# A hybrid decoder step on one core: TensorE's branch for extra pairs ahead of the last pair's second gates, and another order of the last combination

## The chip, the cores and the metric

One core of one Trainium2 chip runs the whole program. The metric is the device time of one execution in microseconds. Before the change three runs took 1240.19, 1240.31 and 1242.56 us; their median is 1240.31 us. The engines are TensorE (PE, its weight loads PEld), VectorE (DVE), ScalarE (ACT), GpSimd (POOL) and SyncE (SP), which here issues the transfers. Each engine has a sequencer that reads its instructions, queues those that the engine executes, and itself executes reads of a register, branches and drains.

## The reference

One step of a decoder layer, for 256 prompt tokens and 32 sample tokens (8 sequences of 4) of width 1024: RMSNorm and one input projection, retention and block-sparse attention beside each other, an output projection and residual, then RMSNorm, a router and 32 experts, of which each token uses 4, another residual, and a last RMSNorm. All of it is in float32. What the change touches is the end of this part:

```python
def expert(acc, xs):
    wgu, bgu, wd, bd, g = xs
    u = tok @ wgu + bgu
    glu = jnp.minimum(u[:, ::2], SWIGLU_LIMIT)
    lin = jnp.clip(u[:, 1::2], -SWIGLU_LIMIT, SWIGLU_LIMIT)
    a = glu * jax.nn.sigmoid(SWIGLU_ALPHA * glu) * (lin + 1.0)
    return acc + g[:, None] * (a @ wd + bd), None
...
return hres + moe(rmsnorm(hres, norm2_g), ...)
...
y_prompt = rmsnorm(yp, final_norm_g)
y_sample = rmsnorm(ys, final_norm_g)
```

## The kernel before

The experts are worked off in 16 pairs. A pair gathers up to 64 tokens for each of its two experts (xt), multiplies them by the gate and up weights ("gates": four parts of 2 MB an expert, 16 matmul instructions a part in the trace), applies the clamped product, and multiplies by the down weights (two parts an expert). The result (out2) is brought back to token rows by a matmul with the weighted one-hot matrix sgt (the combination). SP issues the weight loads, one part of 2 MB each, into a ring of 9 slots; each load waits until the slot's former part has been used.

Pairs 0 to 14 run in a loop on each engine (`pe.Fori` at L1150, three pairs a pass). The last pair has its own function, `last_pair`: the first expert's gates (L1078), the combination of the pair before (`combine`: units 2 and 3 at L955, the sample rows at L959) with the turn of the first expert's product between (`turn_a`, L974), three transposes of the one-hot matrix (L1113), then the second expert's gates (L1078 again, `gates(1)`). What remains is in `finish`: the down matmuls (L1094), the turn of the second expert's product, and `place_y`, which puts part of the residual into PSUM.

If more than 64 tokens chose one expert, extra pairs have to run. Their number is known only on the chip, so every engine reads it (`extra_pairs`, L430 to L433: a wait and a register load from the arena, `TENSOR_LOAD`) and branches on it. On TensorE the branch stands at L1155, between `gates(1)` and `finish`; `finish` is there in both bodies of it. In the run profiled here the number is 0 and the Else body (L1167) is taken.

Behind the branch comes `combine_last`: TensorE adds the last pair's results to the residual in PSUM, in banks of their own. The 32 sample rows are laid as four quarters of 256 columns on 128 rows; their sum of squares is first added up by ScalarE for each quarter, and a matmul with `same_row` (L1005) adds the four quarters of a row. ScalarE squares and adds up (L1486, L1492) and takes roots (`root_last`, L1482); its functions come from table sets, loaded by `ACT_TABLE_LOAD`, which the compiler inserts. VectorE takes the reciprocal (L2007), multiplies by it and by the gains (L2009, L2015), and SP stores: four transfers for the quarters (L2231), one for token tile 0 (L2235), two halves for tile 1 (L2238).

What sets the order: every engine works its own list of instructions, in the order written; semaphores hold an engine until another has come so far. There is no planner.

Of the kernel before, what the change touches and what calls it, by code (L numbers as in the profile page):

```python
# [26 lines left out]
ACT = mybir.ActivationFunctionType  # L27
AXX = mybir.AxisListType.X

P = 128  # L30
D = 1024
# [140 lines left out]
def build_kernel(nc, t, table, outs):  # L172

    with ExitStack() as ctx:
# [7 lines left out]
        psum = ctx.enter_context(nc.psum_tensor("psum", [P, 8, 512], F32))  # L182

        def at(start, *dims):

            flat = arena[:, start:start + int(np.prod(dims))]
            if len(dims) == 1:
                return flat
            names = "abcd"[:len(dims)]
            return flat.rearrange(f"p ({' '.join(names)}) -> p {' '.join(names)}",  # L190
                                  **dict(zip(names, dims)))
# [48 lines left out]
        HT = cur; cur += 2304  # L240
# [54 lines left out]
        f_gain = at(SR + 3072, D)  # L295
# [4 lines left out]
        gain_quarters = at(SR + 2048, 256)  # L300
# [13 lines left out]
        gates = at(MX + 2048 + TILES * (E + 2), TILES, E + 2)  # L314
        assert 2048 + 2 * TILES * (E + 2) <= 2304
        squares = at(HT, D)

        def token_sum(tile):
            a, b = TAIL_BANKS[tile]
            return psum[:, a:b + 1, :]  # L320

        y_out = hn
# [118 lines left out]
        def _(pe):  # L441
# [544 lines left out]
            def combine_last(m):  # L986

                pe.wait_ge(sgt_ready, m + 1)
                pe.wait_ge(out_ready, m * 2 + 1)
                pe.wait_ge(out_half, 1)  # L990
                pe.wait_ge(y_placed, 3)

                def token_tile(tile, half):
                    return mm(psum[:, TAIL_BANKS[tile][half], :], sgt[:, P * tile:P * (tile + 1)],
                              out2[:, 512 * half:512 * (half + 1)], start=False, stop=True,
                              skip_group_check=True)

                for j in range(4):
                    last = mm(psum[NS * j:NS * (j + 1), 0, 0:256], sgt[:, 2 * P:2 * P + NS],
                              out2[:, 256 * j:256 * (j + 1)], start=False, stop=True,  # L1000
                              skip_group_check=True)
                last.then_inc(final_full, 1)
                token_tile(0, 0)
                pe.wait_ge(sq_quarters, 1)
                mm(psum[:, 5, 0:1], same_row, stat[:, 52:53],  # L1005
                   start=True, stop=True).then_inc(final_full, 1)
                token_tile(0, 1).then_inc(final_full, 1)
                token_tile(1, 0)
                token_tile(1, 1).then_inc(final_full, 1)

            def pair(n, landed, ahead):
# [52 lines left out]
            def last_pair(n, landed):  # L1064

                pe.wait_ge(xt_ready, n + 1)
                pe.wait_ge(esel_ready, n + 1)

                def gates(e):
                    lhs = slice(SLOTS * e, SLOTS * (e + 1))  # L1070
                    for kk in range(4):
                        slot, value = landed(4 * e + kk)
                        pe.wait_ge(wt_in[slot], value)
                        for m in range(2):
                            for b in range(2):
                                for g in range(2):
                                    c = 1024 * g + 512 * b
                                    last = mm(psum[64 * g:64 * (g + 1), 6 * e + b, :], xt[:, 2 * kk + m, lhs],  # L1078
                                              gate_slot[slot][:, m, c:c + 512], start=False,
                                              stop=kk == 3 and m == 1, skip_group_check=True)  # L1080
                        last.then_inc(w_used, 1)

                def down(e, q):
                    slot, value = landed(8 + 2 * e + q)
                    if e == 1 and q == 1:
                        pe.wait_ge(half_in, 16)
                    else:
                        pe.wait_ge(wt_in[slot], value)
                    a_t = at_last if e else at_sb
                    for m in range(4):  # L1090
                        if e == 1 and q == 1 and m == 2:
                            pe.wait_ge(wt_in[slot], value)
                        for g in range(2):
                            last = mm(psum[64 * g:64 * (g + 1), 1 if e else 2, :],  # L1094
                                      a_t[:, m, SLOTS * q:SLOTS * (q + 1)],
                                      down_slot[slot][:, m, 512 * g:512 * (g + 1)],
                                      start=q == 0 and m == 0, stop=q == 1 and m == 3)
                    last.then_inc(w_used, 1)

                bias(n, 0)  # L1100
                gates(0)
                pe.wait_ge(sgt_ready, n + 1)
                pe.wait_ge(out_ready, n * 2 + 1)
                combine(n, range(2))
                for b, g in ((0, 0), (1, 1), (0, 1), (1, 0)):
                    mm(psum[64 * g:64 * (g + 1), 6 + b, :], esel[E * b:E * (b + 1), 1, :],
                       bgu[E * b:E * (b + 1), g, :], start=True, stop=False, skip_group_check=True)
                turn_a(n, 0)
                combine(n, range(2, 5))
                pe.wait_ge(selg_ready, n + 1)  # L1110
                pe.wait_ge(u_read, n * 2 + 2)
                for tile in range(3):
                    last = tr(psum[:, 0, P * tile:P * (tile + 1)],  # L1113
                              selg[:, tile].rearrange("p a b -> p (a b)"), ident)
                last.then_inc(sgt_full, 1)
                gates(1)

                def finish():
                    pe.wait_ge(at_ready, n * 2 + 1)
                    down(0, 0)  # L1120
                    turn_a(n, 1)
                    place_y(n + 1, ((0, 0),))
                    down(0, 1)
                    pe.wait_ge(at_ready, n * 2 + 2)
                    down(1, 0)
                    down(1, 1)

                return finish
# [44 lines left out]
        def _(act):  # L1173
# [307 lines left out]
            def root_last(tile, total):  # L1481
                nc.scalar.activation(stat[:, 53 + tile:54 + tile], total, ACT.Sqrt,  # L1482
                                     scale=1.0 / D, bias=const("eps")).then_inc(sq_ready, 1)

            act.wait_ge(final_full, 1)
            nc.scalar.activation(squares[:, 0:256], psum[:, 0, 0:256], ACT.Square,  # L1486
                                 accum_out=stat[:, 52:53]).then_inc(sq_quarters, 1)
            act.wait_ge(final_full, 2)
            root_last(2, psum[:, 5, 0:1])
            for tile in range(2):  # L1490
                act.wait_ge(final_full, 3 + tile)
                link(nc.scalar.activation(squares.rearrange("p (a b) -> p a b", a=2), token_sum(tile), ACT.Square,  # L1492
                                          accum_out=stat[:, 50 + tile:51 + tile]))
                root_last(tile, stat[:, 50 + tile:51 + tile])


        @block.vector
        def _(dve):
# [505 lines left out]
            def final_norm(n, tile, dst, src, gains):  # L2004
                dve.wait_ge(sq_ready, n + 1)
                r = stat[:, 53 + tile:54 + tile]
                v.reciprocal(r, r).then_inc(f_rstd, 1)  # L2007
                dve.wait_ge(f_rstd, n + 1)
                v.scalar_tensor_tensor(dst, src, r, gains, ALU.mult, ALU.mult).then_inc(yo_ready, 1)  # L2009

            halves = lambda a: a.rearrange("p (a b) -> p a b", a=2)
            final_norm(0, 2, y_out[:, 2, 0:256], psum[:, 0, 0:256], gain_quarters)
            final_norm(1, 0, halves(y_out[:, 0, :]), token_sum(0), halves(f_gain))
            final_norm(2, 1, y_out[:, 1, lo], psum[:, TAIL_BANKS[1][0], :], f_gain[:, lo])
            v.scalar_tensor_tensor(y_out[:, 1, hi], psum[:, TAIL_BANKS[1][1], :], stat[:, 54:55], f_gain[:, hi],  # L2015
                                   ALU.mult, ALU.mult).then_inc(yo_ready, 1)
# [89 lines left out]
        def _(sp):  # L2106
# [119 lines left out]
            with sp.Else():  # L2226
                sp.nop()

            sp.wait_ge(yo_ready, 1)
            for j in range(4):  # L2230
                sp.dma_start(outs[1].rearrange("s i d -> (s i) d")[:, 256 * j:256 * (j + 1)],  # L2231
                             y_out[NS * j:NS * (j + 1), 2, 0:256]).then_inc(stored, 16)
            out_p = outs[0][0].rearrange("(t p) d -> p t d", p=P)
            sp.wait_ge(yo_ready, 2)
            sp.dma_start(out_p[:, 0, :], y_out[:, 0, :]).then_inc(stored, 16)  # L2235
            for half in range(2):
                sp.wait_ge(yo_ready, 3 + half)
                sp.dma_start(out_p[:, 1, 512 * half:512 * (half + 1)], y_out[:, 1, 512 * half:512 * (half + 1)])\  # L2238
# [30 lines left out]
```

## Time and profile before

| | |
|---|---|
| profiled execution, in all | 1238.33 us |
| its span | 1236.5 us |
| TensorE matmul, busy | 1195.6 us (97%), 7264 instructions |
| TensorE weight load, busy | 507.2 us (41%) |
| VectorE, busy | 389.5 us (32%) |
| ScalarE, busy | 234.0 us (19%) |
| moved by DMA | 500.64 MB, mean 405 GB/s |
| chain that ended last | TensorE 66%, DMA 21%, VectorE 8%, issue 4%, ScalarE 1% |

Times in the views count from the start of the span. A row of the timeline has start, length, engine, line, operation, output and input, the count of instructions merged into it, and in brackets the idle time before it and what ended it. A matmul's end is modelled, and matmuls overlap, so a group's length is not count times mean. A q behind an engine's name (PEldq, ACTq, SPq) marks its sequencer. The granted clock of TensorE is a share of full speed: 1.00 is 2.4 GHz, 0.50 is 1.2 GHz.

### The profile page before, as it was taken

What the parts mean: (1) busy time and instruction counts of PE and PEld (TensorE: products, weight loads), DVE (VectorE), ACT (ScalarE), POOL (GpSimd) and SP (SyncE); (2) the same over time, 40 slices, a digit from 0 to 9 for tenths busy, and PEclk for the clock granted to TensorE, in tenths of its full rate; (3) what the DMA queues carried; (4) which work ended last, traced back from release to release, by engine and by line L of the source; (5) the groups of instructions that cost most, each with busy time, mean ns of one, the idle gap of its engine ahead of it and who ended that gap; (6) DMA issues with size and microseconds to landing.
All of it is one profiled execution on the core that took longest, in us unless ns stands there. A gap on an engine that the chain in (4) does not pass through costs nothing.

```text
span 1236.5 us, 17233 instructions
## 1 busy us (share of the span) xinstructions
PE 1195.6 (97%) x7264; PEld 507.2 (41%) x7264; DVE 389.5 (32%) x554; ACT 234.0 (19%) x521; POOL 68.0 (6%) x70
## 2 busy tenths in 40 slices
PE   7999999999999999999999999999999999999996
PEld 3555544535443434344343434343343434343432
DVE  4999956464311111222111111112111111111113
ACT  4021145304111101021211101021202111111103
POOL 2222202230000000000000000000000000000000
PEclk9999999999999999999999999999999999999999
DMA  8999889999999999999999999999999999999995
GB/s 333 369 363 361 332 326 389 382 363 385 381 414 427 428 428 428 429 428 428 430 427 430 427 429 428 428 429 428 429 428 429 429 428 430 428 428 430 426 430 233
DMA packets 49978, 500.64 MB, mean 405 GB/s; under 512 B 5656, under 2 KB 6320, under 8 KB 19088
## 3 DMA queue, kind: packets, MB, share of 16 engines
q1 hardware_dynamic: 42416, 430.56, 83.3%
q0 software_dynamic: 7520, 69.47, 14.2%
q8 instruction: 32, 0.52, 0.2%
q14 instruction: 10, 0.08, 0.0%
HBM read 495.29 MB, written 4.72 MB: 404 GB/s over the span
## 4 chain that ended last, share of the span: by engine, by line
PE 66%; DMA 21%; DVE 8%; issue 4%; ACT 1%; SPq 0%; DVEq 0%; ACTq 0%
PE psum L1027 24%; DMA arena<-w_gate_up 18%; PE psum L1058 14%; PE psum L935 6%; DVE arena L1556 5%; DMA arena<-w_down 3%; PE psum L533 3%; PE psum L955 3%; PE psum L941 2%; PE psum L967 2%; PE psum L624 2%; PE psum L753 2%; PE psum L453 2%; PE psum L974 1%; PE psum L1094 1%
## 5 line engine op out<-in xcount | busy, mean ns | idle before, releaser
L1027 PE MATMUL psum<-arena 128*64 128x512 f32 x1920 | 421.7, 594 | 11.8 <-DMA arena<-w_gate_up 11.8
L1027 PEld LDWEIGHTS psum<-arena 128*64 128x64 f32 x1920 | 135.0, 137 | 294.9 <-issue 267.5
L1899 DVE TENSOR_SCALAR arena<-psum 128x512 f32<-128x512 f32 x32 | 22.2, 692 | 675.2 <-PE psum L1027 635.9
L1058 PE MATMUL psum<-arena 128*64 128x512 f32 x960 | 212.6, 595 | 0.0
L1184 ACT ACTIVATE arena<-psum 128x512 f32<-128x512 f32 (+4 forms) x192 | 97.6, 511 | 350.4 <-PE psum L1058 170.6
L1556 DVE STREAM_TRANSPOSE arena<-arena 128x2048 f32<-128x2048 f32 x32 | 121.4, 3926 | 2.1 <-PE psum L518 1.9
L1058 PEld LDWEIGHTS psum<-arena 128*64 128x64 f32 x960 | 66.2, 136 | 124.3 <-issue 122.5
L533 PE MATMUL psum<-arena 128*128 128x512 f32 x224 | 107.7, 618 | 0.4 <-ACT arena L1184 0.4
L1429 ACT ACTIVATE arena<-arena 128x512 f32<-128x512 f32 x30 | 18.9, 631 | 412.5 <-DVE arena L1899 412.5
L1184 ACT ACTIVATE arena<-psum,arena 128x128 f32<-128x128 f32 (+2 forms) x162 | 49.3, 404 | 174.1 <-PE psum L533 113.7
L935 PE MATMUL psum<-arena 128*128 128x128 f32 x512 | 76.8, 293 | 0.2 <-DVE arena L1811 0.2
L935 PEld LDWEIGHTS psum<-arena 128*128 128x128 f32 x512 | 66.4, 199 | 16.7 <-issue 12.7
L955 PE MATMUL psum<-arena 128*128 128x512 f32 x128 | 63.6, 618 | 0.0
L533 PEld LDWEIGHTS psum<-arena 128*128 128x128 f32 x224 | 40.2, 192 | 47.2 <-issue 46.6
L1922 DVE TENSOR_TENSOR arena<-psum,arena 128x512 f32<-128x512 f32 (+1 forms) x80 | 48.0, 633 | 12.6 <-PE psum L955 12.6
L518 PE MATMUL psum<-arena 128*32 128x128 f32 x1024 | 35.4, 280 | 6.7 <-DVE arena L1575 3.8
L518 PEld LDWEIGHTS psum<-arena 128*32 128x32 f32 x1024 | 26.7, 111 | 31.5 <-DVE arena L1556 16.2
L2039 POOL DMA_INDIRECT arena<-cache_k,arena x32 | 32.4, 1011 | 100.8 <-DVE arena L1556 91.9
L967 PE MATMUL psum<-arena 32*64 32x512 f32 x248 | 33.7, 613 | 0.0
L955 PEld LDWEIGHTS psum<-arena 128*128 128x128 f32 x128 | 21.6, 188 | 28.8 <-issue 23.6
L941 PE MATMUL psum<-arena 32*128 32x128 f32 x256 | 32.4, 329 | 0.0
L624 PE MATMUL psum<-arena 128*32 128x512 f32 x256 | 31.2, 605 | 0.0
(261 smaller groups left out, 705.0 us busy)
## 6 DMA issues: line engine op xcount, KB each, us to landing
arena<-w_gate_up SPq DMA_DIRECT2D x128, 2048.0 KB, 31.1
arena<-w_down SPq DMA_DIRECT2D x63, 2048.0 KB, 33.0
arena<-w_in SPq DMA_DIRECT2D x7, 2048.0 KB, 25.1
arena<-w_out SPq DMA_DIRECT2D x2, 2048.0 KB, 12.8
out<-arena POOLq DMA_DIRECT2D x1, 2048.0 KB, 19.5
arena<-w_down SPq DMA_DIRECT2D x2, 1024.0 KB, 38.8
out<-arena SPq DMA_DIRECT2D x3, 512.0 KB, 4.6
arena<-x_prompt SPq DMA_DIRECT2D x2, 512.0 KB, 5.5
```

Source lines behind the costliest of these rows:

```text
L518: last = mm(psum[NS * c:NS * (c + 1), bank, P * (n % 4):P * (n % 4 + 1)], qk[:, g, 4 * c + x, :], kt[:, 4 * c + x, :], start=x == 0, stop= ...
L533: last = mm(psum[:, bank, :], h_t[:, k, tile * P:(tile + 1) * P], w[:, k, :], start=k == 0, stop=k == KC - 1)
L624: last = mm(psum[NS * j:NS * (j + 1), bank, :], pt[:, r, s::4], v_raw(n)[:, r, :], start=half == 0 and r < 4, stop=half == 1 and r >= 4, s ...
L935: mm(o, hn[:, tile, cols], sel[:, tile].rearrange("p a b -> p (a b)"), start=tile == 0, stop=False, skip_group_check=True)
L941: last = mm(o, hn[rows, 2, cols], sel[rows, 2].rearrange("p a b -> p (a b)"), start=False, stop=True, skip_group_check=True)
L955: last = mm(psum[:, 3 + half, :], sgt[:, P * tile:P * (tile + 1)], out2[:, 512 * half:512 * (half + 1)], start=True, stop=True)
L967: mm(psum[64 * g:64 * (g + 1), b, :], esel[E * b:E * (b + 1), e, :], bgu[E * b:E * (b + 1), g, :], start=True, stop=False, skip_group_chec ...
L1027: last = mm(psum[64 * g:64 * (g + 1), b, :], xt[:, 2 * kk + m, lhs], gate_slot[slot][:, m, c:c + 512], start=False, stop=kk == 3 and m == ...
L1058: last = mm(psum[64 * g:64 * (g + 1), 2, :], at_sb[:, m, SLOTS * q:SLOTS * (q + 1)], down_slot[slot][:, m, 512 * g:512 * (g + 1)], start=q ...
L1184: return nc.scalar.activation(out, in_, ACT.Copy, scale=scale)
L1556: v.transpose(kt_sb[:, u % 2, :].rearrange("p (e b r) -> p r e b", e=16, b=32), k_raw[:, u % 4, :]).then_inc(k_trans, 1)
L1922: v.tensor_tensor(dst, got, dst, ALU.add).then_inc(comb_added, 1)
```

## The change

On TensorE the call `gates(1)` moves out of the straight part of `last_pair` into `finish`, and so into both bodies of the branch: reading the number of extra pairs and branching now stand ahead of the second gates, behind the transposes. In `combine_last` the order becomes quarters, tile 0 half, tile 0 half, tile 1 half, same row, tile 1 half. ScalarE squares the quarters into another place of the arena, and takes the quarters' root behind that of tile 0; VectorE scales tile 0 ahead of the quarters, and SP stores them in that order.

```diff
--- before.py
+++ after.py
@@ -1001,11 +1001,11 @@
                               skip_group_check=True)
                 last.then_inc(final_full, 1)
                 token_tile(0, 0)
+                token_tile(0, 1).then_inc(final_full, 1)
+                token_tile(1, 0)
                 pe.wait_ge(sq_quarters, 1)
                 mm(psum[:, 5, 0:1], same_row, stat[:, 52:53],
                    start=True, stop=True).then_inc(final_full, 1)
-                token_tile(0, 1).then_inc(final_full, 1)
-                token_tile(1, 0)
                 token_tile(1, 1).then_inc(final_full, 1)
 
             def pair(n, landed, ahead):
@@ -1113,9 +1113,9 @@
                     last = tr(psum[:, 0, P * tile:P * (tile + 1)],
                               selg[:, tile].rearrange("p a b -> p (a b)"), ident)
                 last.then_inc(sgt_full, 1)
-                gates(1)
 
                 def finish():
+                    gates(1)
                     pe.wait_ge(at_ready, n * 2 + 1)
                     down(0, 0)
                     turn_a(n, 1)
@@ -1483,15 +1483,16 @@
                                      scale=1.0 / D, bias=const("eps")).then_inc(sq_ready, 1)
 
             act.wait_ge(final_full, 1)
-            nc.scalar.activation(squares[:, 0:256], psum[:, 0, 0:256], ACT.Square,
+            nc.scalar.activation(at(HT + D, 256), psum[:, 0, 0:256], ACT.Square,
                                  accum_out=stat[:, 52:53]).then_inc(sq_quarters, 1)
-            act.wait_ge(final_full, 2)
-            root_last(2, psum[:, 5, 0:1])
             for tile in range(2):
-                act.wait_ge(final_full, 3 + tile)
+                act.wait_ge(final_full, 2 + 2 * tile)
                 link(nc.scalar.activation(squares.rearrange("p (a b) -> p a b", a=2), token_sum(tile), ACT.Square,
                                           accum_out=stat[:, 50 + tile:51 + tile]))
                 root_last(tile, stat[:, 50 + tile:51 + tile])
+                if tile == 0:
+                    act.wait_ge(final_full, 3)
+                    root_last(2, psum[:, 5, 0:1])
 
 
         @block.vector
@@ -2009,8 +2010,8 @@
                 v.scalar_tensor_tensor(dst, src, r, gains, ALU.mult, ALU.mult).then_inc(yo_ready, 1)
 
             halves = lambda a: a.rearrange("p (a b) -> p a b", a=2)
-            final_norm(0, 2, y_out[:, 2, 0:256], psum[:, 0, 0:256], gain_quarters)
-            final_norm(1, 0, halves(y_out[:, 0, :]), token_sum(0), halves(f_gain))
+            final_norm(0, 0, halves(y_out[:, 0, :]), token_sum(0), halves(f_gain))
+            final_norm(1, 2, y_out[:, 2, 0:256], psum[:, 0, 0:256], gain_quarters)
             final_norm(2, 1, y_out[:, 1, lo], psum[:, TAIL_BANKS[1][0], :], f_gain[:, lo])
             v.scalar_tensor_tensor(y_out[:, 1, hi], psum[:, TAIL_BANKS[1][1], :], stat[:, 54:55], f_gain[:, hi],
                                    ALU.mult, ALU.mult).then_inc(yo_ready, 1)
@@ -2226,13 +2227,13 @@
             with sp.Else():
                 sp.nop()
 
+            out_p = outs[0][0].rearrange("(t p) d -> p t d", p=P)
             sp.wait_ge(yo_ready, 1)
+            sp.dma_start(out_p[:, 0, :], y_out[:, 0, :]).then_inc(stored, 16)
+            sp.wait_ge(yo_ready, 2)
             for j in range(4):
                 sp.dma_start(outs[1].rearrange("s i d -> (s i) d")[:, 256 * j:256 * (j + 1)],
                              y_out[NS * j:NS * (j + 1), 2, 0:256]).then_inc(stored, 16)
-            out_p = outs[0][0].rearrange("(t p) d -> p t d", p=P)
-            sp.wait_ge(yo_ready, 2)
-            sp.dma_start(out_p[:, 0, :], y_out[:, 0, :]).then_inc(stored, 16)
             for half in range(2):
                 sp.wait_ge(yo_ready, 3 + half)
                 sp.dma_start(out_p[:, 1, 512 * half:512 * (half + 1)], y_out[:, 1, 512 * half:512 * (half + 1)])\
```

## Rows read from the trace of the kernel before

**Rows 1.** Chain of waits, 1100 to the end: start, length, what ran.
```profile
1170.15 36.21 DMA arena<-w_down
```
**Rows 2.** Timeline of the last pair: TensorE from the turn on, one row of VectorE.
```profile
1188.52 0.75 PE L974 MATMUL psum<-arena 128*128 128x128 f32 x4
1189.12 1.99 PE L955 MATMUL psum<-arena 128*128 128x512 f32 x4
1191.04 0.64 PE L959 MATMUL psum<-arena 128*32 128x256 f32 x8
1191.61 0.55 PE L1113 MATMUL psum<-arena 128*128 128x128 f32 x3
1192.08 13.95 PE L1078 MATMUL psum<-arena 128*64 128x512 f32 x64
...
1208.21 0.69 DVE L1908 TENSOR_TENSOR arena<-arena 128x512 f32<-128x512 f32 x1
1208.81 3.66 PE L1094 MATMUL psum<-arena 128*64 128x512 f32 x16 [2.77 <-issue]
...
1214.36 10.52 PE L1094 MATMUL psum<-arena 128*64 128x512 f32 x48
```
**Rows 3.** Sequencers, by line: durations min/median/max in ns, first and last start.
```profile
L433 PEldq TENSOR_LOAD <-arena x1: 491/491/491, 1201.6 to 1201.6; - x1
...
L433 ACTq TENSOR_LOAD <-arena x1: 471/471/471, 1224.9 to 1224.9; - x1
...
L1155 PEldq COMPARE_BRANCH  x1: 6147/6147/6147, 1202.5 to 1202.5; - x1
...
L1150 PEldq COMPARE_BRANCH  x5: 83/215/241, 478.2 to 1165.8; - x5
...
L174 PEldq DRAIN  x1: 3098/3098/3098, 1227.7 to 1227.7; - x1
```
**Rows 4.** One late weight load: its issue, then KB and us to landing.
```profile
1178.18 0.33 SPq L2156 DMA_DIRECT2D arena<-w_down  x1
...
arena<-w_down SPq DMA_DIRECT2D x1, 2048.0 KB, 38.8
```
**Rows 5.** Windows (busy times, then granted clock, DMA share, GB/s); last, TensorE's timeline.
```profile
29.00:29.50 0.50, 0.00 (x0) 0.00 (x0) 0.49 (x4) 0.00 (x0) 0.00 (x0) 0.81 0.98 403
36.00:36.50 0.50, 0.50 (x2) 0.19 (x1) 0.50 (x1) 0.00 (x0) 0.26 (x1) 0.86 1.08 397
1192.00:1198.20 6.20, 6.20 (x32) 2.12 (x32) 0.17 (x1) 0.49 (x1) 0.00 (x0) 1.00 1.05 444
1202.50:1208.60 6.10, 3.54 (x18) 0.94 (x14) 2.38 (x4) 0.63 (x1) 0.00 (x0) 1.00 1.01 424
...
30.72 1.94 PE L518 MATMUL psum<-arena 128*32 128x128 f32 x32 [3.81 <-DVE arena L1575]
```
**Rows 6.** Timeline of the end, all engines, from the last combination on.
```profile
1226.30 1.12 PE L994 MATMUL psum<-arena 128*128 128x512 f32 x2
...
1227.66 1.28 ACT L1482 ACT_TABLE_LOAD   x1
...
1227.94 2.83 PE L994 MATMUL psum<-arena 128*128 128x512 f32 x6
...
1229.11 1.02 ACT L1492 ACTIVATE arena<-psum 128x1024 f32<-128x1024 f32 x1
...
1229.45 0.48 DVE L2009 SCALAR_TENSOR_TENSOR arena<-psum,arena 128x256 f32<-128x256 f32 x1
...
1229.96 1.75 SPq L2231 DMA_DIRECT2D out<-arena  x4
...
1230.78 1.28 DVE L2009 SCALAR_TENSOR_TENSOR arena<-psum,arena 128x1024 f32<-128x1024 f32 x1
...
1232.47 0.75 DVE L2009 SCALAR_TENSOR_TENSOR arena<-psum,arena 128x512 f32<-128x512 f32 x1
...
1233.25 0.99 SPq L2238 DMA_DIRECT2D out<-arena  x2
```

## The prediction

> **What bounds the kernel now.** I read the chain of waits first. Its last transfer is a w_down load that was issued at 1170.15 and landed 36.21 us later, at 1206.36: up to there the stream of expert weights sets the pace, and behind it the engines do [rows 1]. TensorE's timeline of the last pair comes second. Its second gates (L1078, 64 matmuls) run from 1192.08 without a hole, and then TensorE idles 2.77 us "on issue" before the first down matmul (L1094) at 1208.81, though that one's weights lay there from 1206.36 on; from 1208.81 it runs without a hole to 1224.88 [rows 1, 2]. The sequencers' rows say what the hole is. TensorE's sequencer began to read the number of extra pairs at 1201.6, reached the branch (L1155) at 1202.5, and that one instruction took 6147 ns; the five back edges of the pair loop (L1150) took 83 to 241 ns [rows 3]. So a branch whose target had not been met before costs 7.2 us from 1201.6 to 1208.8, and 20 matmuls already queued covered 4.2 us of them.
>
> **What a queued matmul is worth.** 48 and 16 down matmuls take 10.52 and 3.66 us, so each further one costs 0.2144 us [rows 2]. Undisturbed, the 64 gates would hand over after 13.72 us, at 1205.80; the down matmuls began 3.01 us later.
>
> **The branch moves (the main term).** Its instructions stay the same: read, compare, branch. Both bodies now begin with the second gates. What changes is the cover. In the new place, 3 transposes (L1113), 8 small matmuls (L959), 4 (L955) and 4 (L974) stand ahead of it [rows 2]. Counted by the queue alone, the read could start 20 matmuls ahead, near 1188.5. But ahead of L959 TensorE waits for VectorE's third addition, until 1191.04, and the rows speak against a read in front of an open wait. ScalarE's read came at 1224.9, when the wait for the last down matmuls (which ended at 1224.88) opened, with one copy queued in between; and TensorE's closing drain (L174) began at 1227.7, when the wait ahead of the same-row matmul opened, with eight short matmuls behind that wait [rows 2, 3]. So I let the read start at 1191.1, the branch at 1192.0 (0.9 later, as before), and add the same 6.15 us and 0.1: the second gates start at 1198.25 instead of 1192.08, 6.17 us late. The length of the branch is bounded from both sides by rows: 0.08 to 0.24 us as on the back edges, and 6.15 us; I take the upper row, since it is this branch with a target as far off, and the DMA engines are as full in the new stretch (share 1.05, 444 GB/s) as in the old one (1.01, 424 GB/s) [rows 5]. Behind the gates the hole of 3.01 us goes: down(0,0) finds its weights long landed. Net: 6.17 - 3.01 = **+3.2 us** on TensorE.
>
> The Trainium skill has a rule against my reading of the wait ("Perfetto Trace Analysis", Tensor Engine Instruction): an instruction is pushed into a wait queue and the sequencer goes on to the next one before the semaphores are satisfied. By it the read would start near 1188.5; the reads and the drain above do not agree, but they are few, and it is the first rival below.
>
> What is late next: turn_a(1) needs VectorE's product, ready at 1208.90, 3.1 us after the gates hand over [rows 2]; down(0,0) covers 16 x 0.2144 = 3.4 us. That cover was 6.4 us with the hole and is now enough by 0.3 us; I cost it at nothing, at worst 0.5 us. The last loads (one issued at 1178.18 lands 38.8 us later, at 1217.0) come before the later TensorE needs them [rows 4]. SP issues all of them before; nothing in its queue waits for the second gates, whose releases feed no further load.
>
> **The clock.** TensorE now idles 6.1 us, from 1192.15 to 1198.25. In this trace a hole of 3.81 us before 30.72 let the granted clock fall from 1.00 to 0.50 (1.2 GHz) at 29.3, 2.4 us into it, and it rose again at 36.1, 5.4 us after work had resumed; the hole of 2.77 us left it at 1.00 [rows 2, 5]. Half speed for 5.4 us of work would cost 2.7 us, the upper end; the lower is nothing. By the row's 6.8 us at the low level from a fall near 1194.6, the gates would run slow until 1201.4, 3.2 us, and lose 1.6; the fall may come later and last longer into the work, so I take **+1.8 us**.
>
> **The last combination.** Order on TensorE before: quarters, tile 0 half, wait for ScalarE's square of the quarters, same row, other half of tile 0, tile 1. Tile 0 was complete some 0.86 us after 1227.94 and ScalarE squared it from 1229.11, after its second table load (1227.66, 1.28 us) [rows 6]. In old times: now tile 0's four matmuls run from 1226.30 and end near 1228.3, and the same-row matmul no longer waits; TensorE ends near 1230.25 instead of 1230.77. But ScalarE squares tile 0 from 1228.3 to 1229.4, and the table load, which stood between the quarters' square and the first root and lay beside TensorE's work, now stands between tile 0's square and its root: 1229.4 to 1230.7, root at 1231.0, quarters' root 1231.2, tile 1's square to 1232.2, its root 1232.5 (0.3 us later than before). VectorE then does tile 0 first (1.28 us, to 1232.5), the quarters (0.48 us, to 1233.2), and only then tile 1's halves, at 1233.35 instead of 1232.47. SP issues the tile 0 store at 1232.55, then four quarter stores (1.75 us) at 1233.2 to 1235.0, and tile 1's halves queue behind them: the last is issued near 1235.6, before at 1233.9 [rows 6]. What follows that issue (2.6 us to the end of the span) I keep, a little less since the big store is done by then: **+1.6 us**, bounded by +0.4 (no load in the chain) and +2.0.
>
> The Trainium skill ("ScalarE activation tables: per-element evaluation and per-set limits", Table sets in the compiler and the runtime) says that loads are placed per block by the longest run a set can serve. By it one set would serve square and root, and the tail would cost +0.4 us. The trace has a load at 1227.66 between a square and a root, so here it did not come out so [rows 6].
>
> The square into another place of the arena changes no duration: nothing.
>
> **Sum.** 3.2 + 1.8 + 1.6 = +6.6 us on the profiled execution (span 1236.5, in all 1238.33 us): 1244.9. The three timed runs have a median of 1240.31, 2.0 above it; by that measure 1246.9, which I predict.
>
> **Rivals.**
> 1. *The read passes the open wait.* Twenty matmuls ahead it starts near 1188.5 and the gates start at 1195.7, 3.6 us late; less 3.0, TensorE loses 0.6. With a hole of 3.4 us the clock may hold. With the tail +2.2: 1242.5. For it: the lead of 20 matmuls at the old place. Against: ScalarE's read and TensorE's drain [rows 3].
> 2. *The branch is short in its new place* (the side of no loss): if its target is there as on the back edges, the stall goes altogether. TensorE starts down(0,0) at 1206.4, 2.4 us earlier, but reaches down(1,0), before at 1214.36 + 3.43 = 1217.8, ahead of its weights (1217.0): only 0.8 us are won, and the tail takes 1.6. It decides below 1 us of branch: 1241.1, no change. Against: 6147 ns for the same branch under the same DMA load [rows 3, 5].
> 3. *Two fetches follow each other*, since the Else body is longer by the gates: another 6.1 us, less what is queued, and the clock's upper price: 1253.
>
> **How the numbers follow.** Forecast 0.72, rivals 0.14, 0.06, 0.08. The forecast itself spans 1244 to 1250 (branch shorter by 2 or longer by 1.5 us, clock 0 to 2.7, tail 0.4 to 2.0). The range reaches down to the first rival: 1242.3 to 1250.2. 0.2% is 2.5 us, about what a measurement here can tell from no change: slower by more 0.83 (the forecast nearly whole, rival 3, a part of rival 1), within it 0.14 (rivals 1 and 2), faster 0.03: even a free branch does not reach it.
>
> **What would show it.** In the changed kernel: TensorE's read at 1191 and its branch at 1192, near 6 us long; a hole of 6 us before the second gates and none behind them; a granted clock of 0.50 from 1195 to 1202; ScalarE's last table load between tile 0's square and its root; tile 1's stores queued behind four quarter stores. I am wrong if the read starts near 1188, if the branch is far from 6 us, or if the gates start before 1196.

## The result and the profile after

The changed kernel is slower. Its median is 1245.64 us (1243.95 to 1248.4, 11 runs), that of the kernel before, timed beside it, 1240.19 (1238.66 to 1245.82, 11 runs). The ratio on record is 1.0038 with the interval [1.0027, 1.0049], or +4.7 us (3.3 to 6.1); the two medians lie 5.45 us apart, and the text goes by the ratio, which has the interval. The profiled execution of the changed kernel took 1245.64 us with a span of 1243.8.

First the row of TensorE from the page's list of engines (busy time, share of the span, instructions), then the chain of waits (start, length, what ran):

```profile
PE 1198.5 (96%) x7264; PEld 508.3 (41%) x7264; DVE 389.4 (31%) x554; ACT 233.5 (19%) x521; POOL 68.0 (5%) x70
```
```profile
1191.94 6.38 issue
1198.33 16.13 PE psum L1078 x64
...
1234.88 1.28 ACT L1482
...
1236.70 1.28 DVE arena L2010
...
1238.09 0.48 DVE arena L2010
...
1238.68 0.75 DVE arena L2010
```

A busy share of 96% says nothing of the change. The chain does: 6.38 us in which TensorE waited for nothing that the profile shows stand between the transposes (L1113) and the second gates (L1078), where before nothing stood [rows 2]. And ScalarE's table load (L1482) is now in the chain, with VectorE's three products behind it.

TensorE's sequencer, by line (durations min/median/max in ns, first and last start), says what the 6.38 us are:

```profile
L433 PEldq TENSOR_LOAD <-arena x1: 492/492/492, 1191.0 to 1191.0; - x1
...
L1155 PEldq COMPARE_BRANCH  x1: 6437/6437/6437, 1191.8 to 1191.8; - x1
```

The read of the count of extra pairs has moved from 1201.6 to 1191.0 and the branch from 1202.5 to 1191.8. It lasts 6437 ns, 0.29 us more than before [rows 3].

What the branch waits for stands in the view of the DMA queues (queue, packets, MB, share of the 16 engines' time). First the kernel before from 1206.00 to 1206.50, then the changed one from 1195.50 to 1196.00:

```profile
q8 instruction: 1, 0.02, 13.4%
...
q8 instruction: 1, 0.02, 12.7%
```

In each, one packet of 16 KB (the page has 32 of them with 0.52 MB) moves instructions. It starts 3.6 us into the branch before the change and 3.9 us after it, takes 1.07 and 1.02 us (the share of 16 x 0.50 us), and the branch ends 1.4 and 1.5 us after it has landed. This record has eleven branches of more than 3 us, and each has exactly one such packet inside it and ends 1.4 to 1.5 us behind it. Under the weight stream the packet starts 3.5 to 3.9 us into the branch, with the stream over (experiments 4, 5, 7 and 8) 1.0 to 1.5 us. Between 470 and 1160 us, where the pair loop runs and its back edges take 83 to 241 ns [rows 3], this queue moves nothing. So the long branch waits for a transfer of instructions, called the fetch from here on, and what the weight stream adds is the wait until that transfer starts. A packet outside a branch (before: 1197.8, in the middle of the second gates) stops nothing.

The timeline of TensorE from there on, and of the engines at the end (start, busy time, engine, line, operation, tiles, count, idle time before it):

```profile
1190.83 0.64 PE L959 MATMUL psum<-arena 128*32 128x256 f32 x8
1191.40 0.55 PE L1113 MATMUL psum<-arena 128*128 128x128 f32 x3
1198.33 16.13 PE L1078 MATMUL psum<-arena 128*64 128x512 f32 x64 [6.38 <-issue]
...
1214.29 3.60 PE L1094 MATMUL psum<-arena 128*64 128x512 f32 x16
...
1231.16 0.64 PE L999 MATMUL psum<-arena 128*32 128x256 f32 x8 [0.84 <-ACT arena L1184]
1231.72 2.85 PE L994 MATMUL psum<-arena 128*128 128x512 f32 x6
...
1233.75 1.02 ACT L1490 ACTIVATE arena<-psum 128x1024 f32<-128x1024 f32 x1 [0.68 <-PE psum L994]
...
1234.88 1.28 ACT L1482 ACT_TABLE_LOAD   x1
...
1238.02 0.36 SPq L2232 DMA_DIRECT2D out<-arena  x1
...
1238.61 1.97 SPq L2235 DMA_DIRECT2D out<-arena  x4
...
1240.62 0.90 SPq L2239 DMA_DIRECT2D out<-arena  x2
```

Four things are to be seen in it against [rows 2, 6]. The gates start 6.38 us behind the end of the transposes. The 64 gates take 16.13 us, where they took 13.95. The first 16 down matmuls (L1094) follow them with no hole; before, 2.77 us stood there. And at the end ScalarE squares tile 0 (L1490) and only then loads its table (L1482); tile 0's store (L2232) waits for that, the four quarter stores (L2235) follow it, and tile 1's two stores (L2239) are issued last.

Why the gates take longer is in the windows (stretch, sum of busy times, the five engines, granted clock, DMA share, GB/s):

```profile
1195.50:1196.00 0.50, 0.00 (x0) 0.00 (x0) 0.00 (x0) 0.00 (x0) 0.00 (x0) 0.92 0.97 393
1196.00:1196.50 0.50, 0.00 (x0) 0.00 (x0) 0.00 (x0) 0.00 (x0) 0.00 (x0) 0.50 0.92 393
...
1202.50:1203.00 0.50, 0.50 (x4) 0.19 (x2) 0.00 (x0) 0.00 (x0) 0.00 (x0) 0.75 0.98 393
1203.00:1203.50 0.50, 0.50 (x4) 0.14 (x2) 0.00 (x0) 0.00 (x0) 0.00 (x0) 1.00 1.08 459
```

The granted clock falls near 1195.9 from 1.00 (2.4 GHz) to 0.50 (1.2 GHz), in the middle of the idle stretch, and rises near 1202.75, 4.4 us after the gates have started.

The same from one fixed point, the start of the transposes, in both kernels:

| stretch | before | after | difference | forecast |
|---|---|---|---|---|
| transposes to gates (L1113 to L1078) | 0.47 | 6.93 | +6.46 | +6.17 |
| gates to first down (L1078 to L1094) | 16.73 | 15.96 | -0.77 | -3.0 + 1.8 |
| first down to last combination (L1094 to L999) | 16.92 | 16.87 | -0.05 | 0 |
| last combination to the end (L999 to end) | 10.77 | 12.64 | +1.87 | +1.6 |
| sum | | | +7.5 | +6.6 |

In the second row the gates' own +2.18 is the clock, so the hole that went is worth 2.95. The transposes came 0.2 us earlier, which leaves +7.3 for the span (1236.5 to 1243.8).

The traces differ by 7.3 us, the timed runs by 4.7. The profiled execution of the kernel before is one of its shorter ones: 1238.33 us, 1.9 below its median, while that of the changed kernel lies on its median. Less these 1.9 the traces differ by 5.4, inside the interval of the timed runs; the second experiment shows one thing that the executions of the kernel before can differ in. Two more figures bear on it. First, counted from the start of the transposes to the end of the span, the traced difference to the kernel before is larger than the timed one for the changed kernel and for all nine experiments, by 0.7 to 2.8 us (median 1.7). What the ten share is the one trace of the kernel before, so that execution is probably about 1.7 us shorter behind the transposes than its usual one. Second, the clock also differs far ahead of the change: from 252 to 262 us it is granted at 1.00 on average in the kernel before and in experiment 6, at 0.83 or 0.66 in the others.

### The profile page after: what moved, and what is told of

Read it like the earlier page. It is cut to its first block, busy times and chain, and to the rows that moved or that the text cites. A ratio compares the mean times of both kernels' runs of the same rounds, so it can differ in the third digit from the quotient of the medians.

```text
span 1243.8 us, 17233 instructions
## 1 busy us (share of the span) xinstructions
PE 1198.5 (96%) x7264; PEld 508.3 (41%) x7264; DVE 389.4 (31%) x554; ACT 233.5 (19%) x521; POOL 68.0 (5%) x70
## 4 chain that ended last, share of the span: by engine, by line
PE 68%; DMA 19%; DVE 7%; issue 4%; ACT 1%; SPq 0%; DVEq 0%; ACTq 0%; POOLq 0%
PE psum L1027 24%; DMA arena<-w_gate_up 18%; PE psum L1058 14%; DVE arena L1557 5%; PE psum L955 5%; PE psum L935 4%; PE psum L533 3%; PE psum L753 2%; PE psum L967 2%; PE psum L624 2%; PE psum L453 2%; PE psum L1078 2%; PE psum L974 1%; PE psum L941 1%; PE psum L1094 1%
## 5 line engine op out<-in xcount | busy, mean ns | idle before, releaser
L1027 PE MATMUL psum<-arena 128*64 128x512 f32 x1920 | 421.5, 594 | 11.5 <-DMA arena<-w_gate_up 11.5
L1058 PE MATMUL psum<-arena 128*64 128x512 f32 x960 | 212.6, 595 | 0.0
L1078 PE MATMUL psum<-arena 128*64 128x512 f32 x128 | 30.3, 632 | 6.8 <-issue 6.4
```

What stands on the lines that cost most here:

```text
L1027: last = mm(psum[64 * g:64 * (g + 1), b, :], xt[:, 2 * kk + m, lhs], gate_slot[slot][:, m, c:c + 512], start=False, stop=kk == 3 and m == ...
L1058: last = mm(psum[64 * g:64 * (g + 1), 2, :], at_sb[:, m, SLOTS * q:SLOTS * (q + 1)], down_slot[slot][:, m, 512 * g:512 * (g + 1)], start=q ...
```

## The experiments

**1. The branch alone.** Theory: the time is lost by the branch in its new place, and the order of the last combination adds its own part to it. Rival: the order alone.

```diff
                 last.then_inc(sgt_full, 1)
-                gates(1)
                 def finish():
+                    gates(1)
```

> The kernel before with the branch move alone (the last combination in its old order). Theory: the read starts at the opened wait near 1191 and the branch takes about 6.4 us, so the hole in front of the second gates is 6.2 to 6.5 us, the granted clock falls to 0.50 in it and the 64 gates take about 16.1 us; the last combination then starts 5.6 us later than before and keeps its 10.8 us to the end of the span: span +5.6 us. Rival (the move only shifts the hole, and the loss is that of the tail): TensorE reaches the last combination within 1 us of before, and the span grows by less than 1.5 us.

1244.36 us (1243.37 to 1246.91, 7 runs) against 1240.02; ratio 1.0034 [1.0016, 1.0051], +4.2 us. Timeline and sequencer (everything up to the transposes is 2.9 us later in this execution, one of the three with a mean clock of 0.66 from 252 to 262 us):

```profile
1201.05 16.42 PE L1078 MATMUL psum<-arena 128*64 128x512 f32 x64 [5.99 <-issue]
...
1234.17 0.64 PE L999 MATMUL psum<-arena 128*32 128x256 f32 x8 [0.84 <-ACT arena L1184]
```
```profile
L1155 PEldq COMPARE_BRANCH  x1: 6052/6052/6052, 1194.9 to 1194.9; - x1
```

From the transposes (1194.51) to the last combination it takes 39.66 us, as in the changed kernel (39.76) and not as before (34.12); the end takes 10.73, as before (10.77). So the whole of the main term is the one moved line. The length of the branch's bodies is no part of it: with the gates in both it takes 6052 ns here and 6437 in the changed kernel, without them 6147 before [rows 3] and 6107 in experiment 2.

**2. The last combination alone.** The change with that line put back:

```diff
                 last.then_inc(sgt_full, 1)
+                gates(1)
                 def finish():
-                    gates(1)
```

> The kernel before with the new order of the last combination alone (the branch behind the second gates, as before). Theory: from the first matmul of the last combination to the end of the span it takes 12.6 us instead of 10.8: +1.9 us, with a table load between tile 0's square and its root, and tile 1's stores issued behind the four quarter stores. Rival (the new order gains, since TensorE no longer waits for the quarters' square): 0 to -0.7 us.

1240.54 us (1239.75 to 1243.43, 12 runs), ratio 1.0007 [0.9997, 1.0017]. From the last combination to the end 12.61 us, where the changed kernel has 12.64: the traced price of the order, +1.85, comes again. The timed price, +0.9 (-0.4 to 2.1), can't be told from nothing. Its timeline and its windows answer another question:

```profile
1208.57 5.35 PE L1094 MATMUL psum<-arena 128*64 128x512 f32 x16 [2.70 <-issue]
```
```profile
1209.00:1209.50 0.50, 0.50 (x5) 0.18 (x3) 0.50 (x2) 0.00 (x0) 0.00 (x0) 0.90 0.92 393
1209.50:1210.00 0.50, 0.50 (x4) 0.30 (x2) 0.50 (x2) 0.00 (x0) 0.00 (x0) 0.50 1.08 459
...
1212.50:1213.00 0.50, 0.50 (x4) 0.14 (x2) 0.00 (x0) 0.00 (x0) 0.00 (x0) 0.69 1.18 475
```

Up to here this kernel runs the instructions of the kernel before, with its hole behind the gates (2.70 us, there 2.77). This time the clock fell, and the 16 down matmuls took 5.35 us instead of 3.66. So the old order too can lose 1.7 us to the clock, and the traced execution of it did not. In the changed kernel this hole is gone, and with it that loss. How often it falls in the timed runs was not measured; the 1.7 us that the traces of all ten kernels have too much (above) would fit a kernel before that usually loses it, but no second trace of that kernel shows it.

**3. The same branch, with the idle time filled.** Experiment 1, and ahead of the branch ten matmuls of 512 columns that nothing reads (two in each call):

```diff
+                for _ in range(5):
+                    stay_busy(512)
                 def finish():
```

> The branch move alone, with five matmuls that nothing reads (128x512, about 0.86 us each) queued between the transposes and the branch; they run while the sequencer reads and branches. Theory: the branch keeps its 6.4 us and starts no later (fewer than 20 matmul instructions more are queued than fit), so the gates start within 0.3 us of the branch-only kernel's; but TensorE idles only about 2 us, the granted clock stays at 1.00, the gates take 13.9 us instead of 16.1, and the span is 2.2 us shorter than the branch-only kernel's. Rival (the slow gates come from the weight loads or from the code fetch, not from the idle engine): the gates still take about 16 us.

1242.27 us (1240.23 to 1246.37, 12 runs), ratio 1.0021 [1.0007, 1.0034]. Timeline and windows:

```profile
1191.93 4.46 PE L859 MATMUL psum<-arena 128*128 128x512 f32 x10
...
1198.48 15.65 PE L1078 MATMUL psum<-arena 128*64 128x512 f32 x64 [2.09 <-issue]
```
```profile
1199.00:1199.50 0.50, 0.50 (x6) 0.17 (x4) 0.00 (x0) 0.00 (x0) 0.00 (x0) 0.83 1.08 459
```

This missed. The branch took as long (6392 ns from 1192.0), and the filling left 2.09 us of idle time; yet the clock fell, 0.8 us after the gates had begun, and they took 15.65 us. It gave back 0.4 us in the trace (39.28 to the last combination instead of 39.66). Whether the clock is a term at all stayed open, and experiment 9 fills the rest.

**4. The branch behind the last down matmuls.** From the kernel before:

```diff
+            finish()
             with pe.If(more > 0):
-                finish()
...
             with pe.Else():
-                finish()
+                pe.nop()
```

> The kernel before with the down matmuls (finish) taken out of both bodies and put ahead of the branch, so that the branch stands in front of the last combination, where the weight loads are over. Theory: no hole behind the second gates; TensorE's down matmuls end about 0.8 us earlier than before, held by the weights that land near 1217; the read waits for the last weights (about 1222), and the fetch behind the branch, with the DMA engines nearly idle, takes 2 to 3 us instead of 6: span -0.8 to +0.5 us. Rival (the branch takes 6 us whatever the DMA engines do): the last combination starts 3 to 4 us later, span +3 us.

1239.8 us (1237.69 to 1242.85, 12 runs), ratio 1.0003 [0.9991, 1.0015]. Sequencer and timeline:

```profile
L433 PEldq TENSOR_LOAD <-arena x1: 491/491/491, 1220.2 to 1220.2; - x1
...
L1156 PEldq COMPARE_BRANCH  x1: 3350/3350/3350, 1221.1 to 1221.1; - x1
```
```profile
1205.54 3.66 PE L1094 MATMUL psum<-arena 128*64 128x512 f32 x16 [0.48 <-DMA arena<-w_down]
...
1224.80 0.94 PE L999 MATMUL psum<-arena 128*32 128x256 f32 x8 [2.38 <-issue]
```

The last weights were issued at 1181.02 and landed 39.1 us later, at 1220.1; TensorE's read starts at 1220.2, as their wait opens. By its lead of 20 matmuls alone it could have started near 1218.0 (20 x 0.2144 us before the end at 1222.4). That is one more case of a read that doesn't start in front of an open wait. The branch lasts 3350 ns here, with the weight stream over; its packet of instructions starts at 1222.1, 1.0 us into it. The hole behind the gates is gone, but one of 2.38 us opens ahead of the last combination and the clock falls to 0.50 from 1225.0 to 1228.4: what is won on one side goes on the other.

**5. The branch in its old place, but not taken.** The bodies exchanged, so that the usual case (no extra pair) goes straight on:

```diff
-            with pe.If(more > 0):
+            with pe.If(more < 1):
+                finish()
+                combine_last(PAIRS)
+            with pe.Else():
...
-            with pe.Else():
-                finish()
-            combine_last(more + PAIRS)
+                combine_last(more + PAIRS)
```

> The kernel before with the two bodies of TensorE's branch exchanged (the branch asks for fewer than one extra pair), so that without extra pairs it is not taken; the last combination stands in both bodies, and the jump past the other body comes behind it. Place, read and compare are as before. Theory (what costs is the fetch of a target not met before, not the read or the compare): the compare takes under 0.3 us, the hole behind the second gates goes, the down matmuls start when their weights land (0.3 to 0.6 us of wait), and TensorE reaches the last combination 0.6 to 0.9 us earlier than before, held by the weights near 1217; span -0.8 us against the profiled kernel before. Rival (a branch on a value just read costs 6 us whichever way it goes): the hole of 2.7 us stays and so does the time.

1237.92 us (1236.27 to 1240.56, 12 runs) against 1239.94; ratio 0.9988 [0.9978, 0.9998]: faster than the kernel before by 1.5 us (0.2 to 2.7). Sequencer and timeline:

```profile
L1155 PEldq COMPARE_BRANCH  x1: 83/83/83, 1205.3 to 1205.3; - x1
...
L1155 PEldq COMPARE_BRANCH  x1: 3848/3848/3848, 1229.0 to 1229.0; - x1
```
```profile
1209.36 3.65 PE L1094 MATMUL psum<-arena 128*64 128x512 f32 x16 [0.46 <-DMA arena<-w_down]
...
1219.14 7.09 PE L1094 MATMUL psum<-arena 128*64 128x512 f32 x32 [0.57 <-DMA arena<-w_down]
```

The same compare, on the same value, takes 83 ns when it is not taken; the hole behind the gates is gone. What follows waits for w_down, as the second rival had it. The jump past the unused body, 3848 ns from 1229.0, lies beside the end. From the transposes to the last combination it takes 32.76 us instead of 34.12. Of these 1.36, 0.81 are given back at the end (11.58 instead of 10.77), where tile 1's two stores of 256 KB landed in 3.0 us instead of 2.2. Experiment 8, with the same exchanged bodies and the old order, shows the slower end too (11.67), and in experiment 7 the stores take 3.0 us as well. The traces offer a cause, which no run tests: behind the jump these three have a second packet of instructions while the stores run (at 1233.6, 1231.5 and 1235.8), which the kernel before has not, and in their last 0.6 to 1.2 us the stores move at some 25 GB/s, about a sixteenth of the 350 to 390 GB/s ahead of it, as if one of the 16 DMA engines were late.

**6. A root ahead of everything in the last combination.** The changed kernel, and on ScalarE, ahead of the first square, a square root that nothing reads:

```diff
+            nc.scalar.activation(stat[:, 62:63], stat[:, 9:10], ACT.Sqrt, ...)
             act.wait_ge(final_full, 1)
```

> The changed kernel with one more root (of a value that nothing reads) on ScalarE ahead of the quarters' square, so that the table set which serves roots is loaded first. Theory (the table load between tile 0's square and its root is the larger part of what the new order costs): that load goes, tile 0's root comes 1.3 us earlier, and from the first matmul of the last combination to the end of the span it takes 11.4 us instead of 12.6. Rival (the stores' order alone costs it): it still takes 12.4 us or more.

1244.57 us (1242.6 to 1246.52, 6 runs), ratio to the kernel before 1.0038 [1.0024, 1.0051]. Timeline:

```profile
1231.53 1.28 ACT L1485 ACT_TABLE_LOAD   x1 [0.35 <-issue]
...
1235.12 0.29 ACT L1482 ACTIVATE arena<-arena 128x1 f32<-128x1 f32 x1
...
1237.55 1.97 SPq L2236 DMA_DIRECT2D out<-arena  x4
```

One load is left, ahead of the squares; none stands between tile 0's square and its root. The end takes 11.42 us instead of 12.64, so the load was 1.2 of the tail's 1.87. The other 0.65 remain, with the four quarter stores still ahead of tile 1's halves; that they are the price of this order is argued, not shown. The times can't resolve 1.2 us here: the difference to the kernel before lies between 3.0 and 6.3 us.

**7. Everything that looked free.** Experiment 5's branch, the change's order, the root first, and the quarter stores issued from ScalarE's queue:

```diff
+            act.wait_ge(yo_ready, 2)
+            for j in range(4):
+                nc.scalar.dma_start(...)
...
-            for j in range(4):
-                sp.dma_start(...)
```

> The kernel before with the exchanged bodies (branch not taken, behind the second gates), the new order of the last combination, the additional root ahead of it, and the four quarter stores issued by ScalarE's queue instead of SP's. Theory: TensorE reaches the last combination 0.8 us earlier than in the profiled kernel before, and from there to the end it takes 10.3 to 10.5 us instead of 10.8: span -1.2 us, and the timed median 1 to 2.5 us under that of before. Rival (the new order costs because tile 1 is scaled last, whatever queue stores): 11.4 us or more from the last combination to the end, and no gain.

1238.14 us (1236.13 to 1243.36, 12 runs), ratio 0.9985 [0.9974, 0.9996]. Faster than before, but not than experiment 5. The tail missed: 12.53 us. Timeline:

```profile
1235.14 3.04 ACTq L1500 DMA_DIRECT2D out<-arena  x4
...
1235.99 1.70 SPq L2241 DMA_DIRECT2D out<-arena  x2
```

Issued side by side, the four stores take 3.04 us (1.97 on SP alone) and the two 1.70 (0.90), so nothing is won: with the root first (11.42) and the 0.8 to 0.9 us that exchanged bodies cost at the end, 12.2 to 12.3 us would have been expected without this move. That the two queues hold each other up at the issue is likely but not shown: no run has ScalarE issue alone, and experiments 5 and 8, where it issues none, take 1.21 and 1.17 us for the same two stores, with the packet of instructions beside them.

**8. The branch in its new place, but not taken.** Experiment 5, and the moved line of experiment 1. If the place itself cost time (the wait in front of the read, the cover of queued matmuls), this kernel must lose it too; if the fetch behind a taken branch does, it must lose nothing.

```diff
-                gates(1)
                 def finish():
+                    gates(1)
...
-            with pe.If(more > 0):
+            with pe.If(more < 1):
```

> The branch in its new place, ahead of the second gates, but with the two bodies exchanged, so that it is not taken without extra pairs; last combination in its old order, in both bodies. Theory (the loss is the fetch behind a taken branch, and its place only decides how much is covered): the read starts near 1191, the compare takes 0.08 us, the gates start within 0.3 us of where they start in the kernel before, the clock stays at 1.00, and the time is that of the exchanged bodies in the old place, 1237.9 us within 1 us. Rival (the read and the compare themselves hold TensorE in this place, where little is queued): the gates start 1 us late or more, and the kernel is slower than the one with exchanged bodies in the old place by as much.

1238.22 us (1236.22 to 1243.01, 12 runs) against 1240.08; ratio 0.9983 [0.997, 0.9996]. Sequencer and timeline:

```profile
L433 PEldq TENSOR_LOAD <-arena x1: 487/487/487, 1191.4 to 1191.4; - x1
...
L1155 PEldq COMPARE_BRANCH  x2: 83/1823/3563, 1192.3 to 1226.5; - x2
```
```profile
1191.84 0.55 PE L1113 MATMUL psum<-arena 128*128 128x128 f32 x3
1192.42 13.95 PE L1078 MATMUL psum<-arena 128*64 128x512 f32 x64
```

The read starts in the same place behind the same wait (1191.4), the branch at 1192.3 takes 83 ns, and the gates start 0.58 us after the transposes do: 0.11 more than before, instead of 6.46 more. They take 13.95 us at a clock of 1.00. The new place costs a tenth of a microsecond; the taken branch costs the rest. The timed ratio is that of experiment 5 within the intervals.

That a branch is taken isn't enough, though. In the kernel before, ScalarE, VectorE and SyncE read the same count and go to their Else bodies just as TensorE does:

```profile
L1474 ACTq COMPARE_BRANCH  x1: 54/54/54, 1225.7 to 1225.7; - x1
...
L1964 DVEq COMPARE_BRANCH  x1: 67/67/67, 1225.9 to 1225.9; - x1
...
L2219 SPq COMPARE_BRANCH  x1: 50/50/50, 1185.5 to 1185.5; - x1
```

No packet of instructions starts inside these. The body that they pass over is some tens of instructions in the kernel's text, TensorE's hundreds of matmuls. That this length decides is my reading; no run varies it.

**9. The idle time filled whole.** Experiment 3 with seven calls (14 matmuls that nothing reads):

```diff
-                for _ in range(5):
+                for _ in range(7):
                     stay_busy(512)
```

> As the branch-only kernel with matmuls that nothing reads ahead of the branch, now seven (6.0 us) instead of five, so that TensorE idles 0.3 to 0.7 us instead of 2.1. Theory (idle time of TensorE is what lowers the clock): the branch still takes 6.1 to 6.5 us, the granted clock stays at 1.00 through the gates, which take 13.9 us; from the transposes' start to the last combination 37.3 us instead of 39.7 in the branch-only kernel. Rival (the gates run slow for another reason, such as the fetch): the gates take 15.6 us or more, as with five.

1241.85 us (1240.09 to 1245.16, 12 runs), ratio 1.0017 [1.0006, 1.0028]. Timeline and one window:

```profile
1191.44 6.17 PE L859 MATMUL psum<-arena 128*128 128x512 f32 x14
...
1198.30 13.95 PE L1078 MATMUL psum<-arena 128*64 128x512 f32 x64 [0.68 <-issue]
```
```profile
1200.00:1202.00 2.00, 2.00 (x12) 0.72 (x10) 0.00 (x0) 0.00 (x0) 0.00 (x0) 1.00 0.99 418
```

The branch takes as long (6292 ns) and the gates start no earlier (7.24 us after the transposes do, in experiment 1 6.54), but the clock stays at 1.00 and they take 13.95 us instead of 16.42. To the last combination it takes 37.89 us, 1.77 less than in experiment 1: the clock gives back 2.47, and the later start behind the 14 matmuls takes 0.70 of it. The fetch is as long as ever, so it isn't what slows the gates.

## Why the prediction was right, and where its sizes were off

**The branch.** Right, step by step: read at 1191.0 (forecast 1191.1), branch at 1191.8 (1192.0), gates at 1198.33 (1198.25). The transposes were 0.2 us earlier, so the difference is 6.46 and not 6.17: the branch took 6437 ns and not 6147. In its seven taken executions under the weight stream (before, after and experiments 1, 2, 3, 6, 9) it took 6052 to 6437. Experiments 5 and 8 show that it is the taken branch, and not the read, the compare or the place. The reason that I gave, a target not met before, is too wide: the other three engines' branches go to such a target in 50 to 67 ns. What the long ones have is the packet of instructions inside them.

**What is queued as cover.** Right. The wait ahead of L959 holds the read back (1190.83 there, 1191.0 the read), so few matmuls lie ahead of it. The first rival (the read passes the open wait) falls: 1191.0, where by the queue alone it would have been 1188.5, and experiment 4's 1220.2, where it would have been 1218.0. The rule of the Trainium skill behind it ("Perfetto Trace Analysis", Tensor Engine Instruction), that the sequencer goes on before the semaphores are satisfied, isn't what these reads did.

**The hole behind the gates.** Right: 2.95 us went, forecast 3.0. The cover for turn_a(1) held.

**The clock.** Right in kind: the fall came near 1195.9 and not at 1194.6, the low stretch is the 6.8 us of [rows 5], so it reached further into the work and cost 2.2 us instead of 1.8. Experiment 9 takes this term away alone.

**The last combination.** Right in size and in the table load: +1.87 instead of +1.6, of which experiment 6 puts 1.2 on the load between square and root. The other 0.65 I put down to the order of the stores, which fits but wasn't tested alone. The Trainium skill ("ScalarE activation tables: per-element evaluation and per-set limits", Table sets in the compiler and the runtime) has one load by the longest run that a set can serve. The changed kernel has its load at 1234.88 between them all the same; with a root ahead of the squares, one set does serve both (experiment 6).

**From the trace to the median.** This is the step that was off. The terms add to +6.6 and the trace shows +7.3, but I put them on the median of the kernel before, as if its slower executions lost something that the change keeps. Put on the profiled execution they give 1244.9, and the median came out at 1245.64. Experiment 2 shows one loss that the change does not keep: 1.7 us of clock behind the old hole. By the timed runs the change costs 4.7 us (3.3 to 6.1), less than the 6.6 of the sum and the 7.3 of the traces. The range would have held from either starting point; what I had wrong is what the usual execution of the kernel before already loses.

**The other rivals.** The second, a short branch, is not what happened, but experiments 5 and 8 built it: 1.36 us to the last combination in the one, 1.33 in the other, where I had priced 0.8. The third, two fetches, falls: one branch row, one hole, one packet of instructions in it; the next packet (1201.5) comes while the gates run and stops nothing.

## What to carry to other kernels

A branch that jumps over a long body can stall its engine for microseconds while instructions are fetched (here 6 us under the weight stream, 3.4 to 3.9 without it), while going straight on cost 0.08 us, and the jumps over short bodies 0.05 to 0.07: let the usual case go straight on and put the rare body behind the jump. Count the jump past the rare body too: it stood at the end here. If a branch must be taken, look at which wait ends last ahead of it: what is queued between that wait and the branch is all the cover there is. And work put in another order changes where a table load falls and which store is last in the queue; price both.

## What was not expected of the hardware

- The branch is long even without the weight stream: 3350 to 3883 ns in experiments 4, 5, 7 and 8, against 6052 to 6437 under it. The difference is the time until the packet of instructions starts (1.0 to 1.5 us against 3.5 to 3.9); behind the packet it is 1.4 to 1.5 us in all.
- The fall of the clock is not settled by the length of one hole: it came with 2.09 us (experiment 3) and 2.70 (experiment 2), in both some 0.8 us after work had resumed, and not with 2.77 [rows 2]. What decides stayed open.
- Stores issued at once from ScalarE's and SP's queues took longer at the issue (3.04 and 1.70 us, where SP alone took 1.97 and 0.90).
- With exchanged bodies and the old order of the last combination (experiments 5 and 8) the end took 11.58 and 11.67 us, before 10.77. The packet of instructions beside the stores (experiment 5) is a likely cause; it was not tested.
